# The sample tile's expert rows: eight single-row transfers on each of the SP and ACT queues in place of two indirect transfers on GpSimd

## The chip, the cores and the metric

The kernel runs on one core of one Trainium2 chip. The metric is the device time of one execution in microseconds (us); lower is better.

## The reference, cut to what matters

One inference step of a decoder trunk with two layers, for 512 prompt tokens and 8 sample tokens that share every weight, all in float32, model width 1024. Each layer is a mixer (mLSTM in layer 0, differential attention over a paged cache in layer 1, memory attention beside both), an output projection, a layer norm, a hierarchical mixture of 16 experts and a second layer norm. The change touches only what lies around the experts:

```python
ffn = hier_moe(x, w_group, b_group, w_router, b_router, w_e1, w_e3, w_e2)
return layer_norm(ALPHA * x + ffn, ln_ffn_g, ln_ffn_b)

def hier_moe(...):
    lg = xt @ w_group + b_group                      # 4 groups
    g = argmax(lg); p_g = softmax(lg)[g]
    le_g = (xt @ w_router + b_router)[group g]       # 4 experts of the group
    vals, idx = top_k(le_g, 2)
    wk = softmax(vals) * p_g                         # two experts a token, with weights
    h = silu(xt @ w1[e]) * (xt @ w3[e])
    y = sum over the two chosen e of wk * (h @ w2[e])
```

## The kernel before, in words

The 520 tokens lie in SBUF in `X` as five tiles of the token rows: tiles 0 to 3 are the prompt's, 128 rows each, and tile 4 (`PT`) is the samples' with 8 rows. `ORDER` is `[4, 0, 1, 2, 3]`, so that the samples' tile comes first wherever tiles are walked. Five engines each run their own list of instructions in written order (PE, VectorE or DVE, ScalarE or ACT, GpSimd or POOL, and SyncE or SP, which only issues transfers), and semaphores tie them together. The program is cut into blocks, and all five engines meet between two blocks: nobody begins the next block before the last one has ended this one.

The stages of a layer that matter here:

- **Routing** (`route(l, R)`, a block of its own). DVE works out, for each token, the two rows (`SLU`, `q` = 0 and 1) of a DRAM buffer `XS` in which the token's vector is wanted, since `XS` is ordered by expert, and raises `slot_ready`. GpSimd then scatters the five tiles of `X` to `XS` with ten indirect transfers, two for each tile (L1209), each of which counts into `xs_out`. ACT and DVE meanwhile work out the weights `WT2` of the two experts: ACT takes two exponentials (L1193, L1195), and DVE ends with L1309 to L1315. In layer 0 the same block also holds the memory keys and values of layer 1: PE multiplies them, ACT copies four banks out (L1200) and a transposed one (L1202), and SP stores them to DRAM (L1157, L1158) once four copies are there (`mem1_out`), and waits for these two stores (`mem1_kept`) at the end of its block.
- **Experts** (`experts(l, R)`, in the next block). ACT waits for `xs_out` and then loads `XS` in groups of 128 rows (`rows_in`, L1398). PE transposes each group (L1348), multiplies it with the experts' weights (L1359, L1381), and the results go to a second DRAM buffer `YS`.
- **Combination** (`combination(l, R)`). When every row of `YS` is written, ACT raises `y_all` (L1530). SP then loads the norm's scale and shift (`GB`, L1566), GpSimd gathers the tokens' rows back from `YS` into `YG` with ten indirect transfers (L1572), two for each tile in the order of `ORDER`, each pair counting into `ys_in[t]`. For each tile ACT scales the first row by its weight (`weigh`, L1580), DVE adds both rows to the residual (`residual`, L1625 to L1628), ACT takes the deviation (`deviation`, L1587, L1588) and DVE applies the norm (`normed`, L1635 to L1637). DVE's order is residual(0), residual(1), normed(0), residual(2), normed(1), and so on; ACT's is weigh(0), weigh(1), deviation(0), weigh(2), deviation(1), and so on, and index 0 is the samples' tile.

After the combination of layer 0 the same block goes on with layer 1: PE first turns the samples' tile and projects it, then the prompt's tiles, and the SP queue loads weights and cache pages (L1922, L1940, L1947). After the combination of layer 1 only the stores of the output are left.

## Time and profile before

| | us |
|---|---|
| median of 3 runs | 1326.72 |
| the three runs | 1319.88, 1326.72, 1330.5 |
| the profiled execution, its own time | 1322.12 |
| its span in the trace | 1320.3 |
| PE busy | 1101.7 (83% of the span) |
| DVE busy | 395.9 (30%) |
| ACT busy | 259.8 (20%) |
| POOL busy | 57.7 (4%) |

PE is busy most of the time, and the moments in which it is not are the places where the change acts: around the two scatters and the two combinations. The busy share of an engine therefore says little here; what counts is the wait that ends last at each of these four places.

### The profile page before, as it was taken

To read this page: it belongs to the slowest core of one execution; us is meant where nothing else is said; L and a number is where in the kernel's file an instruction comes from. 1 tells how busy PE (TensorE), PEld (TensorE's weight loads), DVE (VectorE), ACT (ScalarE), POOL (GpSimd) and SP (SyncE) were. 2 spreads that over 40 slices of the span, in tenths; PEclk is the share of its full clock that TensorE was granted. 3 is DMA by queue.
4 is the path that set the end of the run, shared out by engine and by line. 5 is a ranking of instruction groups with operands and counts; after the bars stand their busy time and mean duration, and the time that the engine had idled before them with its cause. 6 is when DMAs were issued, how large, how long until landed. Compare 5 with 4: busy or idle time off the path is not lost. (4 is left out here: it accounts for less than half of the span.)

```text
span 1320.3 us, 22081 instructions
## 1 busy us (share of the span) xinstructions
PE 1101.7 (83%) x8836; PEld 689.5 (52%) x8836; DVE 395.9 (30%) x1034; ACT 259.8 (20%) x686; POOL 57.7 (4%) x75
## 2 busy tenths in 40 slices
PE   7899999968994999917999888998876993699860
PEld 5688888854454333306887755554543442233210
DVE  2132223333534111136010023344333336011118
ACT  2122222113011111133110022223342101111014
POOL 4000000000002000030000000000000002000012
PEclk9999999979998899968999889999877997799885
DMA  9944442155626999999999955999623704899934
GB/s 335 407 151 120 120 120 81 45 172 227 272 103 246 343 400 410 339 337 319 356 351 351 340 178 186 351 358 353 251 106 119 287 0 186 312 374 374 420 127 187
DMA packets 131414, 333.91 MB, mean 253 GB/s; under 512 B 9951, under 2 KB 67472, under 8 KB 121710
## 3 DMA queue, kind: packets, MB, share of 16 engines
q1 hardware_dynamic: 115630, 274.98, 57.8%
q0 software_dynamic: 9200, 34.39, 6.6%
q10 hardware_dynamic: 6480, 23.10, 4.5%
q8 instruction: 71, 1.16, 0.3%
q14 instruction: 33, 0.27, 0.1%
HBM read 288.25 MB, written 44.19 MB: 252 GB/s over the span
## 5 line engine op out<-in xcount | busy, mean ns | idle before, releaser
L1359 PE MATMUL bank<-W,XT 128*32 128x512 f32 x1408 | 160.9, 610 | 6.3 <-DMA W<-in_w13f 3.9
L2141 PE MATMUL bank<-XT,W 128*128 128x260 f32 x448 | 113.1, 409 | 4.7 <-DVE CAT L2399 3.2
L1071 PE MATMUL bank<-WOUT,CAT 128*128 128x512 f32 x256 | 111.6, 594 | 0.0
L2141 PEld LDWEIGHTS bank<-XT,W 128*128 128x128 f32 x448 | 88.5, 203 | 27.6 <-issue 8.2
L1359 PEld LDWEIGHTS bank<-W,XT 128*32 128x32 f32 x1408 | 44.9, 113 | 106.8 <-issue 103.2
L485 PE MATMUL bank<-XT,WH 128*128 128x260 f32 x448 | 100.0, 384 | 0.0
L485 PEld LDWEIGHTS bank<-XT,WH 128*128 128x128 f32 x448 | 84.5, 190 | 13.3
L485 PE MATMUL bank<-WH,XT 128*128 128x256 f32 x384 | 84.0, 379 | 0.0
L1381 PE MATMUL bank<-WD,GT 128*32 128x512 f32 x704 | 80.0, 595 | 1.6 <-DVE GT L1455 1.6
L1071 PEld LDWEIGHTS bank<-WOUT,CAT 128*128 128x128 f32 x256 | 48.0, 190 | 57.9 <-issue 57.8
L485 PEld LDWEIGHTS bank<-WH,XT 128*128 128x128 f32 x384 | 72.5, 190 | 10.0 <-issue 0.4
L1348 PE MATMUL bank<-C,CAT 128*128 128x128 f32 x176 | 25.8, 293 | 42.0 <-DMA CAT<-XS 42.0
L1447 DVE TENSOR_TENSOR XT<-bank,XT 128x256 f32<-128x256 f32 x22 | 9.3, 424 | 161.0 <-ACT XT L1422 161.0
L1992 PE MATMUL bank<-PGS,QD 128*32 128x128 f32 x1536 | 48.6, 279 | 6.1 <-DMA PGS<-in_KP 6.1
L1348 PEld LDWEIGHTS bank<-C,CAT 128*128 128x128 f32 x176 | 20.3, 148 | 59.2 <-DMA CAT<-XS 42.5
L2081 PE MATMUL bank<-PGS,CAT 128*32 128x384 f32 x512 | 47.3, 491 | 4.2 <-DMA PGS<-in_VP 4.2
L1992 PEld LDWEIGHTS bank<-PGS,QD 128*32 128x32 f32 x1536 | 41.5, 112 | 14.1 <-issue 12.6
L2141 PE MATMUL bank<-WV,XT 128*128 128x256 f32 x192 | 45.8, 394 | 1.7 <-ACT XT L987 1.7
L1381 PEld LDWEIGHTS bank<-WD,GT 128*32 128x32 f32 x704 | 20.8, 109 | 45.7 <-issue 43.7
L1209 POOL DMA_INDIRECT XS<-X,SLU x20 | 19.0, 949 | 524.8 <-DVE SLU L1292 519.3
L2141 PEld LDWEIGHTS bank<-WV,XT 128*128 128x128 f32 x192 | 36.8, 196 | 8.0 <-ACT XT L987 1.8
L1422 ACT ACTIVATE XT<-bank 128x256 f32<-128x256 f32 x22 | 8.5, 385 | 157.9 <-PE bank L1359 157.9
(401 smaller groups left out, 1275.5 us busy)
## 6 DMA issues: line engine op xcount, KB each, us to landing
W<-in_w13f SPq DMA_DIRECT2D x32, 2048.0 KB, 12.7
PGS<-in_KP SPq DMA_DIRECT2D x128, 384.0 KB, 5.2
PGS<-in_VP SPq DMA_DIRECT2D x128, 384.0 KB, 5.2
WD<-in_w2f SPq DMA_DIRECT2D x32, 1024.0 KB, 13.6
WH<-in_w_a SPq DMA_DIRECT2D x13, 1024.0 KB, 11.1
CAT<-XS ACTq DMA_DIRECT2D x22, 512.0 KB, 10.0
XS<-CAT POOLq DMA_DIRECT2D x19, 512.0 KB, 15.5
WOUT<-in_w_out SPq DMA_DIRECT2D x4, 2048.0 KB, 13.1
```

The lines of the kernel that those rows point to most:

```text
L485: last = nc.tensor.matmul(PB[u["bank"]][:, 0:u["w"]], u["lhsT"](w, k), u["rhs"](w, k), start=(k == 0), stop=(k == KC - 1))
L1071: last = nc.tensor.matmul(PB[2 * (i % 2) + c][:, :], CAT[:, k, t * P:(t + 1) * P], w_out(c)[:, k, :], start=(k == 0), stop=(k == KC - 1))
L1209: nc.gpsimd.indirect_dma_start(XS, bass.IndirectOffsetOnAxis(ap=SLU[0:rows(t), q, t:t + 1], axis=0), X[0:rows(t), t, :], None).then_inc(xs ...
L1348: last = nc.tensor.transpose(PB[k // 4][:, (k % 4) * P:(k % 4 + 1) * P], XG[:, g % 3, k * P:(k + 1) * P], ident)
L1359: last = nc.tensor.matmul(PB[2 + g % 2][32 * j:32 * j + 32, :], XGT[:, g % 2, k, 32 * j:32 * j + 32], W13[:, LANES[l][g][j] % WRING, k, :] ...
L1381: last = nc.tensor.matmul(PB[5 + c][32 * j:32 * j + 32, :], GT[:, g % 2, k, 32 * j:32 * j + 32], WD2[:, LANES[l][g][j] % WRING, k, c * 512 ...
L1422: nc.scalar.activation(SIL[:, g % 2, :], PB[2 + g % 2][:, 0:FE], ACT.Silu).then_inc(s_ready, 1)
L1447: nc.vector.tensor_tensor(GA[:, g % 2, :], PB[2 + g % 2][:, FE:2 * FE], SIL[:, g % 2, :], ALU.mult).then_inc(g_ready, 1)
L1992: last = nc.tensor.matmul(bank[32 * j:32 * j + 32, q * P:(q + 1) * P], QD[:, i, 4 * g + j, :], page[:, j, i, :], start=(i == 0), stop=(i = ...
L2081: last = nc.tensor.matmul(PB[6 + c][32 * j:32 * j + 32, 0:384], weight, v, start=(p == 0), stop=(p == PAGES))
L2141: last = nc.tensor.matmul(PB[u["bank"]][0:u["m"], 0:u["w"]], u["lhsT"](w, k), u["rhs"](w, k), start=(k == 0), stop=(k == KC - 1))
```

## The change

The samples' tile leaves GpSimd. Its 16 rows (8 tokens, two experts each) are moved by 16 plain transfers of one row of 4 KB, eight on SP (q = 0) and eight on ACT (q = 1), whose DRAM row is a number that the engine has read from `SLU` into a register. GpSimd keeps the eight indirect transfers of the four full tiles, at the scatter and at the gather. New semaphores `xs_rows` and `ys_rows` count the single rows; who waited for `xs_out` or `ys_in[4]` now waits for these. The wait for the norm's scale and shift (`ln_in`) moves from ahead of residual(0) to ahead of normed(0).

The first `sample_rows` stands in `route`, the second in `combination`:

```diff
+            def sample_rows(eng, q):
+                eng.wait_ge(slot_ready, l + 1)
+                for b in range(NB):
+                    slot = eng.value_load(SLU[b:b + 1, q, PT:PT + 1], min_val=0, max_val=ROWS - 1)
+                    eng.dma_start(XS[bass.ds(slot, 1), :], X[b:b + 1, PT, :]).then_inc(xs_rows[q], 16)
...
                 def _(sp):
+                    sample_rows(sp, 0)
                     if l == 0:
                         sp.wait_ge(mem1_out, 4)
...
                 def _(act):
+                    sample_rows(act, 1)
                     act.wait_ge(rt_exp, 2 * l + 1)
...
                     pool.wait_ge(slot_ready, l + 1)
-                    for t in ORDER:
+                    for t in range(PT):
...
-                act.wait_ge(xs_out, 160 * (l + 1))
+                act.wait_ge(xs_out, 32 * PT * (l + 1))
+                for q in range(2):
+                    act.wait_ge(xs_rows[q], 16 * NB * (l + 1))
...
+            def sample_rows(eng, q):
+                slots = [eng.value_load(SLU[b:b + 1, q, PT:PT + 1], min_val=0, max_val=ROWS - 1) for b in range(NB)]
+                eng.wait_ge(y_all, l + 1)
+                for b, slot in enumerate(slots):
+                    eng.dma_start(YG[b:b + 1, 0, q, :], YS[bass.ds(slot, 1), :]).then_inc(ys_rows[q], 16)
...
             def on_sp(sp):
-                sp.wait_ge(y_all, l + 1)
+                sample_rows(sp, 0)
                 for c, name in enumerate(("ln_ffn_g", "ln_ffn_b")):
...
                 for i, t in enumerate(ORDER):
-                    for q in range(2):
+                    for q in range(2 if t < PT else 0):
...
-                    act.wait_ge(ys_in[t], 32 * (l + 1))
+                    rows_in(act, t)
...
+                sample_rows(act, 1)
                 weigh(0)
...
-                dve.wait_ge(ln_in, 64 * (l + 1))
                 residual(0)
                 for i in range(NT):
                     if i + 1 < NT:
                         residual(i + 1)
+                    if i == 0:
+                        dve.wait_ge(ln_in, 64 * (l + 1))
                     normed(i)
```

The next four listings show the order of instructions. In them `SLU_2710` is layer 0's `SLU`, `T_0_2692` the input of the first exponential, `SW_0_2700` that of the second, and ISA stands for register operations.

ACT in layer 0's routing block, before; the two copies from `bank` to XT and the two to MEMV are the memory keys and values:

```order
L1190 UNCONDITIONAL_BRANCH [waits barrier_Pool_Activation_PE_DVE_SP_release]
L1193 ACT_TABLE_LOAD
L1193 ACTIVATE T_0_2692<-T_0_2692 128x20 [waits rt_exp]
L1195 ACTIVATE SW_0_2700<-SW_0_2700 128x5 [waits rt_done]
L1200 ACTIVATE XT<-bank 128x256 [waits mem1_ready] x2
L1200 ACTIVATE MEMV<-bank 128x256 [waits mem1_ready] x2
L1202 ACTIVATE MEMKT<-bank 128x512 [waits mem1_ready]
```

The same place after the change, with the pair of value_load and transfer shown once of the eight times that it stands there:

```order
L1201 UNCONDITIONAL_BRANCH [waits barrier_Pool_Activation_PE_DVE_SP_release]
L1159 TENSOR_LOAD SLU_2710 [waits slot_ready]
L1159 ISA x2
L1160 ISA
L1160 DMA XS<-X 1x1024
...
L1205 ACT_TABLE_LOAD
L1205 ACTIVATE T_0_2692<-T_0_2692 128x20 [waits rt_exp]
L1207 ACTIVATE SW_0_2700<-SW_0_2700 128x5 [waits rt_done]
```

All eight rows, and the load of the activation table too, now stand between `slot_ready` and ACT's first exponential; the four copies for which SP's stores wait come behind them.

ACT from the end of layer 0's experts into its combination, before; L1530 is the instruction that raises `y_all`, and the tile YG is named YG_2939:

```order
L1530 ACTIVATE SW_0_2700<-SW_0_2700 1x1
L1580 ACTIVATE YG_2939<-YG_2939,WT_0_2711 8x1024 [waits ys_in4]
L1580 ACTIVATE YG_2939<-YG_2939,WT_0_2711 128x1024 [waits ys_in0]
L1587 ACTIVATE YG_2939,LNSF_2941<-X,LNSF_2941 8x1024 [waits var_ready]
L1588 ACT_TABLE_LOAD
```

After, where the value_load stands eight times and then the transfer eight times:

```order
L1544 ACTIVATE SW_0_2700<-SW_0_2700 1x1
L1585 TENSOR_LOAD SLU_2710
L1585 ISA x2
...
L1588 ISA [waits y_all]
L1588 DMA YG_3163<-YS 1x1024
...
L1607 ACTIVATE YG_3163<-YG_3163,WT_0_2711 8x1024 [waits ys_rows1,ys_rows0]
L1607 ACTIVATE YG_3163<-YG_3163,WT_0_2711 128x1024 [waits ys_in0]
```

On ACT the eight value_loads stand behind the instruction that raises `y_all`. On SP, which doesn't raise it, they stand ahead of the wait for it.

## Rows read from the trace of the kernel before

**Rows 1.** The list of waits: engine, line, awaited work; total us, times, longest

```profile
PE bank L1348 <- DMA CAT<-XS: 42.0, 2, 25.9
```

**Rows 2.** Timeline, layer 1, scatter: start, length, engine, line, operation, idle before

```profile
1112.70 0.17 DVE L1292 CAST SLU<-SW 128x10 uint32<-128x10 f32 x1
...
1113.19 0.95 POOL L1209 DMA_INDIRECT XS<-X,SLU  x1 [143.99 <-DVE SLU L1292]
...
1115.87 0.17 DVE L1309 TENSOR_REDUCE SW<-T 128x5 f32<-128x20 f32 x1
...
1117.03 0.17 DVE L1315 TENSOR_TENSOR WT<-WT,SW 128x5 f32<-128x5 f32 x1
...
1124.48 0.96 POOL L1209 DMA_INDIRECT XS<-X,SLU  x1 [0.30 <-issue]
1129.96 1.32 ACTq L1398 DMA_DIRECT2D CAT<-XS  x3
```

**Rows 3.** The stretches by windows, busy time of each engine, clock, DMA share, GB/s

```profile
421.00:424.00 3.00, 0.00 (x0) 0.00 (x0) 0.00 (x0) 0.00 (x0) 0.30 (x1) 0.50 1.01 388
```

**Rows 4.** SP's L1932 in 582.3 to 586 us, by source line

```profile
L1932 SPq TENSOR_LOAD <-PG x4: 260/274/283, 582.4 to 584.1; - x4
```

**Rows 5.** Timeline of SP, 614 to 616 us

```profile
614.22 1.90 SPq L1940 DMA_DIRECT2D PGS<-in_KP  x4
```

**Rows 6.** L1940 over the span, by source line: issue ns, and issue to landing

```profile
L1940 SPq DMA_DIRECT2D PGS<-in_KP x128: 332/333/2817, 591.7 to 750.4; - x128
...
DMA to landing us min/median/max: 3.0/5.2/10.5
```

**Rows 7.** Timeline, layer 0, scatter, columns as in rows 2

```profile
396.76 1.28 ACT L1193 ACT_TABLE_LOAD   x1 [0.57 <-PEq L1042]
...
408.58 0.17 DVE L1292 CAST SLU<-SW 128x10 uint32<-128x10 f32 x1
...
409.64 0.64 ACT L1200 ACTIVATE XT<-bank 128x256 f32<-128x256 f32 x2
...
410.17 0.38 ACT L1200 ACTIVATE MEMV<-bank 128x256 f32<-128x256 f32 x1
...
414.38 0.69 SPq L1158 DMA_DIRECT2D out_mem_v<-MEMV  x1
...
420.35 0.95 POOL L1209 DMA_INDIRECT XS<-X,SLU  x1 [0.30 <-issue]
426.88 1.31 ACTq L1398 DMA_DIRECT2D CAT<-XS  x3
```

**Rows 8.** L1158, the store of the memory values, issue to landing

```profile
DMA to landing us min/median/max: 6.4/6.4/6.4
```

**Rows 9.** Timeline, layer 1, combination, columns as in rows 2

```profile
1281.61 0.20 ACT L1530 ACTIVATE SW<-SW 1x1 f32<-1x1 f32 x1 [4.90 <-DMA YS<-CAT]
...
1287.97 1.15 ACT L1580 ACTIVATE YG<-YG,WT 8x1024 f32<-8x1024 f32 x1 [6.17 <-DMA YG<-YS,SLU]
...
1291.82 0.14 DVE L1628 TENSOR_SCALAR LNSF<-LNSF 8x1 f32<-8x1 f32 x1
...
1292.34 1.23 DVE L1625 SCALAR_TENSOR_TENSOR X<-X,YG 128x1024 f32<-128x1024 f32 x1 [0.39 <-ACT YG L1580]
...
1294.68 0.29 ACT L1588 ACTIVATE LNSF<-LNSF 8x1 f32<-8x1 f32 x1
...
1295.01 0.15 DVE L1635 RECIPROCAL LNSF<-LNSF 8x1 f32<-8x1 f32 x1
```

**Rows 10.** Timeline, layer 0, combination, columns as in rows 2

```profile
572.48 0.20 ACT L1530 ACTIVATE SW<-SW 1x1 f32<-1x1 f32 x1 [5.71 <-DMA YS<-CAT]
...
581.55 1.15 ACT L1580 ACTIVATE YG<-YG,WT 8x1024 f32<-8x1024 f32 x1 [8.87 <-DMA YG<-YS,SLU]
...
589.05 0.15 DVE L1635 RECIPROCAL LNSF<-LNSF 8x1 f32<-8x1 f32 x1
...
591.87 1.01 PE L979 MATMUL bank<-C,X 8*128 8x8 f32 x8 [25.77 <-DVE X L1637]
```

More of the change, by code:

```diff
@@ L1138, in _ @@
                             norm_steps(nc, dve, t, n0 + i, LNS, GB)
+        xs_rows = [sem("xs_rows0"), sem("xs_rows1")]
+        ys_rows = [sem("ys_rows0"), sem("ys_rows1")]
         rt_exp, rt_done, rk_in, rk_ready, slot_ready, xs_out = (
@@ L1561, in combination, with rows_in @@
             SLU, WT2 = R["SLU"], R["WT2"]
+            def rows_in(eng, t):
+                if t < PT:
+                    eng.wait_ge(ys_in[t], 32 * (l + 1))
+                else:
+                    for q in range(2):
+                        eng.wait_ge(ys_rows[q], 16 * NB * (l + 1))
+            def sample_rows(eng, q):
[3 more added lines that the diff above has]
+                    eng.dma_start(YG[b:b + 1, 0, q, :], YS[bass.ds(slot, 1), :]).then_inc(ys_rows[q], 16)
             def on_sp(sp):
-                sp.wait_ge(y_all, l + 1)
+                sample_rows(sp, 0)
                 for c, name in enumerate(("ln_ffn_g", "ln_ffn_b")):
@@ L1619, in residual @@
                     st = LNS[0:r, n % 2, :]
-                    dve.wait_ge(ys_in[t], 32 * (l + 1))
+                    rows_in(dve, t)
                     dve.wait_ge(y_weighed, NT * l + i + 1)
```

## The prediction

> **What bounds the kernel now.** I read the list of waits first. PE is the engine that does most of the work, so a change in a side path counts only where PE, or at the very end DVE, stands still for it. Twice, for 42.0 us together, PE waits for the first group of rows to come from XS, which can only be read when the scatter has landed [rows 1]. The timelines of the two scatters and the two combinations then show what ends last there. The four places are independent, so the result is the sum of four shifts.
>
> In layer 1's scatter the slots are ready at 1112.87 (the cast of 1112.70 and its 0.17). GpSimd issues its first transfer at 1113.19 and its tenth at 1124.48, one each 1.25 us, and ACT may issue the first load of XS at 1129.96 [rows 2]: 5.5 us behind the start of the tenth. In layer 0 the tenth is at 420.35 and the load at 426.88 [rows 7]; the DMA engines carry 388 GB/s between them [rows 3]. In the combinations the first thing that waits is ACT's scaling of the samples' tile, at 1287.97 and at 581.55; both end an idle time of ACT that was spent on the gather [rows 9, 10].
>
> **What one row costs.** The trace has both halves of it on SP. Four value_loads begin between 582.4 and 584.1, so one takes 1.7/3 = 0.57 us, of which the TENSOR_LOAD itself is 0.27 [rows 4]. Four transfers with an address in a register take 1.90 us; less the last one's 0.33, a third of the rest is 0.52 us each [rows 5, 6]. A scattered row therefore costs 1.09 us of its queue, eight rows 8.7 us. In the gather the loads come first (8 x 0.57 = 4.6 us) and then the transfers (seven steps of 0.52 = 3.6 us up to the start of the last). I take ACT to be as fast as SP; no row shows it. Against this, GpSimd needs 2 x 1.25 = 2.5 us for both transfers of the same tile.
>
> How soon a row of 4 KB lands is not in the trace. The shortest landing of L1940, of 384 KB, is 3.0 us and the median 5.2, in which the DMA engines are loaded [rows 6]. I take 3.0 where the queues are quiet and 4.0 where they are full.
>
> The Trainium skill, page "DMA: Bandwidth & Descriptors", speaks against this change: its section "Rules for kernel authors" says to coalesce many small transfers into one, since under 64 KB most of the time is overhead, and its section "Latency and other measured facts" puts the floor of a register load from a tensor at about 600 ns. The trace agrees with the second figure (0.57 us a value_load); with 0.6 for 0.57 the sum below would rise by 0.2 us in each combination.
>
> **Scatter, layer 1: -2.5 us.** GpSimd begins with tile 0 at once, so all eight full transfers and their data move 2.5 us forward: the last is issued at 1122.0 and the load of XS at 1127.4 [rows 2]. What must be over by then: the rows on both queues end at 1112.87 + 8.7 = 1121.6 and land 3 to 4 us later, 1125.6. ACT loads its activation table behind its rows (it did so at 396.76 in layer 0, during its wait, 1.28 us [rows 7]), and has its first exponential at about 1123.1. DVE's part that needs it took from 1115.87 to 1117.20, so 1.3 us [rows 2]; it ends at 1124.5. All this is covered by the landing of the scatter, with 2.9 us to spare for the slowest queue. If the drain of the data and not the issue set the end, nothing would be won; the bounds are -2.5 and 0, and I take -2.5, because GpSimd's first full tile is what starts the data.
>
> **Scatter, layer 0: 0 us.** GpSimd's side again ends 2.5 us earlier, at 424.4. But here the stores of layer 1's memory keys and values stand behind the rows. Step by step: slots ready 408.75; ACT's rows to 417.5; the table 1.28, to 418.8. From slots ready to the first copy, two exponentials included, it took 409.64 - 408.75 = 0.9, so the copies begin at 419.7; four of them are 0.64 + 0.38 + 0.38 = 1.4, to 421.1 [rows 7]. SP can then issue its two stores, the second some 0.5 us later (an estimate: one issue of 0.33 and a gap), at 421.6; in the trace it was issued at 414.38 and landed 6.4 us later in the midst of the scatter [rows 7, 8]. SP waits for it before the block may end. With 6.4 us the block ends at 428.0, with L1940's 3.0 at 424.6; half of the scatter's tail still lies beside it, so I take the middle, 4.7: 426.3, and 0.4 for the change of block. That is 426.7 against 426.88, no gain. Bounds: -2.5 if the store is hidden, +1.5 with its old landing.
>
> **Combination, layer 0: +2.6 us.** `y_all` comes from ACT's instruction at 572.48. Only behind it ACT does its eight value_loads, to 577.0, and begins the last row at 580.7 [rows 10]; SP has its loads done before and is 4 us ahead, so ACT is late. The DMA engines are full here: landed at 584.7, against the start of the scaling at 581.55, +3.1 us. From there to the reciprocal of the samples' tile it took 589.05 - 581.55 = 7.5 us, in layer 1 only 1295.01 - 1287.97 = 7.0 [rows 9, 10]; the 0.5 was tile 0's late arrival, and that is gone, since tile 0 is gathered 2.5 us earlier. PE starts on the samples' tile directly behind this norm, at 591.87 [rows 10], and all that follows hangs on it. DVE's later tiles follow in the same order and shift as well.
>
> **Combination, layer 1: +4.8 us.** Here the end of the kernel hangs on it. ACT's instruction is at 1281.61; loads to 1286.2, the last row begun at 1289.8, landed at 1292.8, against 1287.97 [rows 9]. DVE's first residual ends 4.0 us behind the scaling's start (1291.96), and before the change DVE then stood 0.4 us for tile 0 (1292.34); the deviation ends at 1294.97 and releases the reciprocal at 1295.01 [rows 9]. Behind the samples' tile all later tiles of DVE stand in a dense row, so the whole end moves: +4.8. The upper bound is a landing of 5.2 (+7), the lower one a value_load that costs its TENSOR_LOAD alone and transfers at 0.33, 8 x 0.27 + 7 x 0.33 = 4.5 us in place of 8.2: +1.1.
>
> **Without cost.** The wait for the norm's scale and shift: SP issues these loads about 4.2 us later (8 x 0.52), behind its rows. They are needed only by the first norm, which begins some 7 us after the scaling, so the move of the wait hides them. SP's loads behind them in layer 0 (WV, the pages) also start 4 us later into DMA engines that are full anyway.
>
> **Sum.** 0 - 2.5 + 2.6 + 4.8 = +4.9 us. Against the profiled execution's own time, 1322.12, that is 1327.0. That execution lies 4.6 below the median of 1326.72, and the mean of all four is 1324.8; on that I forecast **1330 us**, 0.4% slower.
>
> **Rivals.**
>
> *The samples' tile doesn't pace the combination.* If rows on ACT are as cheap as the lower bound and land at once, tile 0, which comes 2.5 us earlier, helps instead: -0.5 in layer 0 and -0.4 in layer 1 from the gaps that it left, and -2.5 in each scatter. Sum -5.9: 1319. For it: the engines' idle time before the scaling (8.9 and 6.2 us) was all wait for a transfer [rows 9, 10]. Against it: the loads are serial and behind `y_all`.
>
> *The scatter is bound by its drain.* The DMA engines carry 388 GB/s in the tail [rows 3], and one full tile of 512 KB each 1.25 us is 419 GB/s: more than they take. If the data and not the issue sets the end, GpSimd's 2.5 us come out of a queue that is full anyway, layer 1 gives 0 and layer 0 +1.5: sum +8.9, 1334.
>
> *Issuing a row is dearer than 0.52 us.* One issue of L1940 took 2.8 us where 0.33 is usual [rows 6], so an issue can be held up, and the rows are issued by SP and ACT at once while GpSimd's tiles flow. If a row's transfer costs p, each combination grows by 7(p - 0.52) and layer 0's scatter by 8(p - 0.52); layer 1's has 2.9 us to spare. At p = 0.9 the sum passes +13 us, the bound below; at p = 1.0 it is 4.9 + 6.7 + 3.8 + 0.9 = +16: 1341. Against it: the median of 128 issues is the shortest, 0.33.
>
> The Trainium skill, page "Perfetto Trace Analysis", section "DMA Instruction — HWDGE (DVE, Sync)", says that one descriptor generator is locked by one sequencer at a time and that this lock's wait is inside the profiled length. If SP and ACT share it, two streams of 0.33 us every 1.09 us (the scatter) fit into each other, and the sum stays.
>
> *The change does nothing.* Not possible for GpSimd's share; the four shifts could cancel to 0: 1325, inside the forecast's own range.
>
> **Chances.** The forecast (with what cancels) 0.57, drain-bound 0.18, not pacing 0.13, dear issue 0.12. A measurement of this kernel can tell about 1% from no change (the runs shown spread by 0.8%). 1% is 13.2 us: faster by that needs more than every gain in this sum, 0.03; slower by it is most of the last rival, 0.10; the rest, 0.87, is within. The range takes in the first rival and the second and stops short of the last: 1317 to 1340; of this, some 4 us at either end are the spread of the runs.
>
> **What would show it.** In the profile after: GpSimd's eighth indirect transfer 8.8 us behind its first at all four places; the rows of ACT 1.1 us apart in the scatter; ACT's load of XS at slots ready + 14.5 in layer 1 (17.1 before), and in layer 0 SP's end of the block released by the store of the memory values. In the combinations ACT's scaling of the samples' tile 11.2 us behind the start of ACT's L1530 in layer 1 (6.4 before) and 12.2 in layer 0 (9.1 before), released by a row, with tile 0 already there. I am wrong if ACT's value_loads cost clearly less than 0.57, if a row lands in under 2 us, or if the load of XS doesn't move in layer 1.

## The result, and the profile after

| | before | after |
|---|---|---|
| median of the runs, us | 1325.91 (4 runs, 1319.88 to 1330.5) | 1343.47 (4 runs, 1339.0 to 1347.73) |
| ratio after/before | | 1.0126, 95% interval 1.008 to 1.0171 |
| profiled execution, its own time | 1322.12 | 1347.73 |
| its span | 1320.3 | 1345.9 |
| PE busy / POOL busy | 1101.7 / 57.7 | 1109.8 / 48.4 |

The change makes the kernel 1.3% slower, 17.6 us; the forecast was 1330 us, 0.4% slower. The profiled execution is the slowest of its four, so its span of +25.6 us has to be taken apart. Length of each stretch in the two profiles, in us:

| stretch | before | after | difference | forecast |
|---|---|---|---|---|
| to layer 0's slots | 408.75 | 408.72 | 0.0 | 0 |
| layer 0, slots ready to PE's first group | 21.34 | 23.39 | +2.1 | 0 |
| layer 0, experts | 142.39 | 142.86 | +0.5 | 0 |
| layer 0, ACT's instruction behind the last store to PE on the samples' tile | 19.39 | 24.27 | +4.9 | +2.6 |
| from there to layer 1's slots | 521.00 | 530.39 | +9.4 | 0 |
| layer 1, slots ready to PE's first group | 20.54 | 20.24 | -0.3 | -2.5 |
| layer 1, experts | 148.20 | 149.88 | +1.7 | 0 |
| layer 1, ACT's instruction to the end of DVE's last norm | 35.66 | 43.12 | +7.5 | +4.8 |

The four places of the change give +14.1 us, each of them above its term. The 9.4 us between the layers can't be put down to the change: a second run of the same kernel had 513.96 there (E4 below).

The list of waits of the kernel after; columns as in [rows 1].

```profile
PE bank L1360 <- DMA CAT<-XS: 31.8, 2, 25.6
...
PE bank L979 <- DVE X L1665: 30.4, 1, 30.4
```

PE's wait for the rows of XS fell from 42.0 us [rows 1] to 31.8, and yet neither scatter won anything to speak of. In layer 0 the idle time is only split in another way: PE now stands 11.4 us for ACT's copy of the memory keys, which comes behind ACT's rows (row 424.81 of layer 0's scatter, below), does 1.1 us of transposes, and then stands 6.2 for XS. A group of waits that shrinks is no gain until the end of its stretch has moved. The second row grew by 4.6 us, and that is real [rows 10].

The timeline of layer 1's combination after, against [rows 9]:

```profile
1299.75 0.20 ACT L1544 ACTIVATE SW<-SW 1x1 f32<-1x1 f32 x1 [5.16 <-DMA YS<-CAT]
1300.13 3.21 SPq L1588 DMA_DIRECT2D YG<-YS  x8
1300.22 0.98 POOL L1599 DMA_INDIRECT YG<-YS,SLU  x1 [160.24 <-ACT SW L1544]
...
1304.16 3.28 ACTq L1588 DMA_DIRECT2D YG<-YS  x8
...
1308.98 0.94 POOL L1599 DMA_INDIRECT YG<-YS,SLU  x1 [0.30 <-issue]
1313.65 2.19 ACT L1607 ACTIVATE YG<-YG,WT 8x1024 f32<-8x1024 f32 x2 [13.70 <-DMA YG<-YS]
...
1320.61 0.15 DVE L1663 RECIPROCAL LNSF<-LNSF 8x1 f32<-8x1 f32 x1 [0.30 <-ACT LNSF L1615]
```

ACT's loads take 4.41 us (1299.75 to 1304.16), its rows 3.05 to the start of the last (1307.21), and then 6.44 us pass until the scaling. "x2" says that ACT scales the samples' tile and tile 0 without a gap: GpSimd's first full tile was there by the time ACT was free for it. The chain of waits has the same as "1307.21 6.36 DMA YG<-YS". From the scaling to the reciprocal it is 6.96 us, as before (7.04), and all later tiles follow. SP's loads of the norm's scale and shift are issued just ahead of ACT's rows and among them:

```profile
1303.38 0.37 SPq L1593 DMA_DIRECT2D GBF<-in_ln_ffn_g  x1
1304.10 0.36 SPq L1593 DMA_DIRECT2D GBF<-in_ln_ffn_b  x1
```

Layer 0's combination, the same view, against [rows 10]:

```profile
574.97 0.20 ACT L1544 ACTIVATE SW<-SW 1x1 f32<-1x1 f32 x1 [5.42 <-DMA YS<-CAT]
...
579.39 3.82 ACTq L1588 DMA_DIRECT2D YG<-YS  x8
...
589.46 2.19 ACT L1607 ACTIVATE YG<-YG,WT 8x1024 f32<-8x1024 f32 x2 [14.29 <-DMA YG<-YS]
...
599.24 1.02 PE L979 MATMUL bank<-C,X 8*128 8x8 f32 x8 [30.36 <-DVE X L1665]
```

The loads and the transfers of ACT's rows by source line (ns: shortest, median, longest):

```profile
L1585 ACTq TENSOR_LOAD <-SLU x16: 275/277/292, 575.0 to 1303.5; - x16
...
L1588 ACTq DMA_DIRECT2D YG<-YS x16: 226/235/510, 579.4 to 1307.2; - x16
```

In the gather the price of a row is as forecast or under it: a load each 0.55 us, a transfer each 0.41 in layer 1 and 0.48 in layer 0. In the scatter it is not. Layer 1's timeline after, against [rows 2]:

```profile
1129.46 0.17 DVE L1304 CAST SLU<-SW 128x10 uint32<-128x10 f32 x1
...
1130.52 12.52 ACTq L1160 DMA_DIRECT2D XS<-X  x8
...
1139.04 0.95 POOL L1221 DMA_INDIRECT XS<-X,SLU  x1 [0.30 <-issue]
1143.07 1.28 ACT L1205 ACT_TABLE_LOAD   x1 [26.08 <-issue]
1144.37 0.22 ACT L1205 ACTIVATE T<-T 128x20 f32<-128x20 f32 x1
...
1144.69 0.17 DVE L1321 TENSOR_REDUCE SW<-T 128x5 f32<-128x20 f32 x1 [12.05 <-ACT T L1205]
...
1145.75 0.17 DVE L1327 TENSOR_TENSOR WT<-WT,SW 128x5 f32<-128x5 f32 x1
1146.51 1.34 ACTq L1410 DMA_DIRECT2D CAT<-XS  x3
```

GpSimd's last transfer is issued 9.4 us behind the slots, where it was 11.6: of its forecast 2.5 us, 2.2 are there. But ACT's eight rows end 13.4 us behind the slots instead of 8.7; table, exponential and DVE's six steps on the weights stand behind them; and the block can't end until DVE is through. ACT's load of XS comes 16.9 us behind the slots (17.1 before). Layer 0 the same way, against [rows 7]:

```profile
409.64 12.93 ACTq L1160 DMA_DIRECT2D XS<-X  x8
...
422.60 1.28 ACT L1205 ACT_TABLE_LOAD   x1 [26.47 <-issue]
...
424.81 1.12 PE L1198 MATMUL bank<-C,XT 128*128 128x128 f32 x4 [11.36 <-ACT XT L1212]
...
425.79 0.48 SPq L1169 DMA_DIRECT2D out_mem_v<-MEMV  x1
...
428.80 1.35 ACTq L1410 DMA_DIRECT2D CAT<-XS  x3
```

The store of the memory values is issued at 425.79, 4.2 us later than I had it, lands 2.5 us later, and the block ends on it: the load is at 428.80, against 426.88.

### The profile page after: what moved, and what is told of

It is laid out like the page before. It is cut to its first block and busy times, and to the rows that moved or that the text cites. A ratio compares the mean times of both kernels' runs of the same rounds, so it can differ in the third digit from the quotient of the medians.

```text
span 1345.9 us, 22467 instructions
## 1 busy us (share of the span) xinstructions
PE 1109.8 (82%) x8836; PEld 692.9 (51%) x8836; DVE 396.2 (29%) x1034; ACT 259.0 (19%) x686; POOL 48.4 (4%) x67
## 3 DMA queue, kind: packets, MB, share of 16 engines
q10 hardware_dynamic: 6544, 23.24, 4.4%
q8 instruction: 71, 1.16, 0.3%
## 5 line engine op out<-in xcount | busy, mean ns | idle before, releaser
L2170 PE MATMUL bank<-XT,W 128*128 128x260 f32 x448 | 116.1, 417 | 4.7 <-DVE CAT L2428 3.2
L1360 PE MATMUL bank<-C,CAT 128*128 128x128 f32 x176 | 25.8, 293 | 31.8 <-DMA CAT<-XS 31.8
L2021 PEld LDWEIGHTS bank<-PGS,QD 128*32 128x32 f32 x1536 | 41.4, 112 | 16.8 <-issue 13.5
L979 PE MATMUL bank<-C,X 128*128 128x128 f32 (+1 forms) x120 | 16.0, 275 | 30.4 <-DVE X L1665 30.4
## 6 DMA issues: line engine op xcount, KB each, us to landing
W<-in_w13f SPq DMA_DIRECT2D x32, 2048.0 KB, 13.4
XS<-CAT POOLq DMA_DIRECT2D x19, 512.0 KB, 15.4
```

What stands on the lines that cost most here:

```text
L979: last = nc.tensor.transpose(PB[4 + 2 * (n % turns) + k // 4][:, (k % 4) * P:(k % 4) * P + r], X[0:r, t, k * P:(k + 1) * P], const("ident" ...
L1360: last = nc.tensor.transpose(PB[k // 4][:, (k % 4) * P:(k % 4 + 1) * P], XG[:, g % 3, k * P:(k + 1) * P], ident)
L2021: last = nc.tensor.matmul(bank[32 * j:32 * j + 32, q * P:(q + 1) * P], QD[:, i, 4 * g + j, :], page[:, j, i, :], start=(i == 0), stop=(i = ...
L2170: last = nc.tensor.matmul(PB[u["bank"]][0:u["m"], 0:u["w"]], u["lhsT"](w, k), u["rhs"](w, k), start=(k == 0), stop=(k == KC - 1))
```

## The experiments

Medians and ratios of all of them first; a ratio is given where there were several rounds, the rest are single runs.

| run | this, us | before in the same job, us | ratio, 95% interval |
|---|---|---|---|
| E1 scatter only | 1323.74 | 1323.4 | 0.9995, 0.9965 to 1.0025 |
| E2 gather only | 1336.81 | 1323.4 | 1.009, 1.0059 to 1.0121 |
| E3 before again | 1325.77 | 1323.4 | 0.9995, 0.9957 to 1.0033 |
| E4 after again | 1338.55 | 1323.4 | 1.012, 1.0049 to 1.0191 |
| E5 GpSimd's gather behind the rows | 1347.13 | 1326.21 | |
| E6 ACT's loads before the last stores | 1334.46 | 1326.21 | |
| E7 scatter only, exponentials first | 1327.09 | 1326.21 | |
| E8 scatter only, loads first | 1321.5 | 1326.21 | |
| E9 change with E6 and E7 | 1331.69 | 1322.43 | 1.0061, 1.0031 to 1.0091 |
| E10 scatter only, tiles held | 1334.53 | 1322.43 | |
| E11 scatter only, one queue | 1343.27 | 1322.43 | |
| E12 layer 1's scatter only | 1321.11 | 1322.43 | 0.9995, 0.9966 to 1.0023 |
| E13 as E9, loads inside the experts | 1327.5 | 1324.58 | 1.0022, 0.9999 to 1.0045 |
| E14 scatter only, tiles held, loads first | 1335.69 | 1324.58 | |
| E15 scatter only, tiles held, one queue | 1358.05 | 1324.58 | |

Single times of one kernel spread by 8 to 23 us, so the length of a stretch in each profile is the finer measure: scatter (slots to PE's first group) and combination (ACT's instruction to PE, or to DVE's last norm), in us.

| run | scatter 0 | combination 0 | between | scatter 1 | combination 1 |
|---|---|---|---|---|---|
| before | 21.34 | 19.39 | 521.00 | 20.54 | 35.66 |
| E3 | 21.43 | 19.59 | 521.09 | 20.33 | 35.80 |
| after | 23.39 | 24.27 | 530.39 | 20.24 | 43.12 |
| E4 | 23.48 | 24.28 | 513.96 | 20.24 | 43.65 |
| E1 | 23.24 | 19.34 | 518.95 | 19.44 | 35.75 |
| E2 | 21.29 | 24.16 | 525.32 | 20.31 | 43.10 |
| E5 | 23.57 | 29.66 | 524.77 | 20.26 | 44.27 |
| E6 | 23.14 | 19.14 | 524.26 | 20.05 | 37.53 |
| E7 | 22.06 | 19.48 | 524.16 | 19.05 | 35.76 |
| E8 | 22.22 | 19.40 | 519.22 | 20.47 | 35.69 |
| E9 | 22.21 | 19.36 | 524.17 | 19.05 | 38.39 |
| E12 | 21.36 | 19.61 | 520.81 | 19.12 | 36.04 |
| E13 | 22.13 | 19.02 | 528.50 | 19.16 | 37.76 |

### E1 to E4: the halves apart, and both kernels again

E1 takes the gather back (and the place of the wait for the norm's scale and shift with it), E2 the scatter; E3 and E4 are the kernels before and after, unchanged.

```diff
 E1
-                sample_rows(act, 1)        # in the combination, and on SP
-                    for q in range(2 if t < PT else 0):
+                    for q in range(2):
 E2
-                    sample_rows(act, 1)    # in the router, and on SP
-                    for t in range(PT):
+                    for t in ORDER:
```

> Only the two scatters are changed; the two combinations are as before. In the profiles, from the slots to PE's first group the changed kernel took 23.4 and 20.2 us, before 21.3 and 20.5. Theory A (the loss is the sum of the four places): the same two lengths again, +2 us in all, ratio 1.001 to 1.002, and PE's stretch from layer 0's combination to layer 1's slots 521 us as before. Rival B (the scatter change costs something elsewhere, since the stretch between the combination of layer 0 and the slots of layer 1 was 9 us longer in the profile after): +8 us or more, ratio 1.006 or more.

> Only the two gathers and the place of the wait for the norm's parameters are changed; the scatters are as before. Theory A: the combinations take 4.9 and 7.5 us longer than before, as in the profile after, so +12 us, ratio 1.009. Rival B: the gather change also lengthens the stretch after it, +17 us or more, ratio 1.013.

> The kernel before, profiled a second time, to see how much the lengths of stages vary from run to run. Theory A: the four changed places within 0.5 us of the first profile, while the stretch from layer 0's combination to layer 1's slots, where PE's granted clock fell to 0.73 and 0.83 in two windows, may vary by some 5 us on its own. Rival B: this stretch is 521 us again within 1 us, so that the 9 us in it belong to the change. Ratio 1.000.

> The changed kernel, profiled a second time. Theory A: 23.4, 24.3, 20.2 and 43.1 us at the four places again (within 0.5), and the stretch from layer 0's combination to layer 1's slots anywhere from 521 to 530. Rival B: that stretch is 530 us again. Ratio 1.010 to 1.014 in either case.

The whole measurable loss is the gather's: E2 costs 0.9%, some 12 us, and its two combinations are longer by 4.8 and 7.4, 12.2 together. E1 costs nothing that can be measured; its stretches give +1.9 and -1.1. The combinations repeat within 0.6 us from run to run. The stretch between the layers doesn't: E3 had the 521 us again that I had named as the sign of the rival, but E4, the changed kernel, had 514.0 where it first had 530.4, below all that I had expected. Over all 17 profiles it is 514.0 to 530.4.

A good part of the difference between the two profiles of the changed kernel is TensorE's clock. For the same 4151 matmuls of the stretch PE is busy for 456.6 us at a mean granted clock of 0.91 in the first and for 447.0 at 0.93 in E4, 9.6 of the 16.4 us. In the first, 40 us of it (999 to 1039) stand at 0.59, so mostly at the lower of the two levels, 1.2 and not 2.4 GHz; at the same place E4 has 0.87. Why the clock fell there in one run and not in the other stays open. Nor is it shown that the change has no part in this stretch: the seven profiles with the changed gather have 524.5 us on average, the ten others 520.7, a difference well inside their spread. E2's time, 12 us longer where its two combinations account for 12.2, speaks against a large one.

### E5 and E6: why a row lands so late

Theory: ACT's rows wait in the DMA engines behind the full tiles that GpSimd issues at the same time. Rivals: a row is slow by itself, or takes a constant 6.4 us. E5 lets GpSimd begin only when the rows have landed. E6 moves ACT's eight value_loads ahead of its wait for the last stores, so that the rows go out with fewer tiles ahead of them.

```diff
 E5
                 pool.wait_ge(y_all, l + 1)
+                for q in range(2):
+                    pool.wait_ge(ys_rows[q], 16 * NB * (l + 1))
 E6
                 count, done = number(act)
+                R["slots"] = [act.value_load(R["SLU"][b:b + 1, 1, PT:PT + 1], ...) for b in range(NB)]
                 for u in range(2):
                     act.wait_ge(y_stored[u], stored[u])
```

> The changed kernel, with GpSimd's gather of the four full tiles held back until the sixteen rows have landed. In both profiles after, ACT began the samples' tile 14.5 and 13.9 to 14.4 us behind L1544, of which the last row was issued at 7.5. Theory A (a row lands late because it is queued behind the full tiles that GpSimd issues at the same time): without them the last row lands 2 to 3 us behind its issue, so ACT begins at 9.5 to 10.5 us. Rival B (single rows are slow by themselves: 16 of them in 13.4 us, one after the other, 0.84 us each): ACT begins at 13.9 us again. In both the full tiles come later, so the combinations as a whole get longer; their length tells nothing.

> The changed kernel, with ACT's eight value_loads of the gather ahead of its wait for the last stores of YS, so that its rows are issued from L1544 on, 4.3 us earlier. Theory A (rows queue behind GpSimd's tiles): the last row is issued at about 3.9 us with three tiles' transfers ahead of it in place of six, and lands some 3 to 5 us later, so ACT begins at 7 to 9 us in place of 14, and the combinations are 5 us shorter. Rival B (rows are slow by themselves): the sixteen rows still take 13 us from the first issue, ACT begins at 13 to 14 us. Rival C (only ACT's lateness counts and the delay in the queue is constant, 6.4 us): ACT begins at 9.7 us, 4.3 earlier.

The timeline of E5, layer 1. GpSimd's first transfer now comes behind the scaling:

```profile
1298.00 0.20 ACT L1544 ACTIVATE SW<-SW 1x1 f32<-1x1 f32 x1 [4.91 <-DMA YS<-CAT]
...
1302.41 3.28 ACTq L1588 DMA_DIRECT2D YG<-YS  x8
1308.08 1.15 ACT L1609 ACTIVATE YG<-YG,WT 8x1024 f32<-8x1024 f32 x1 [9.88 <-DMA YG<-YS]
1308.83 0.98 POOL L1601 DMA_INDIRECT YG<-YS,SLU  x1 [169.77 <-DMA YG<-YS]
```

E6, layer 1:

```profile
1291.98 0.20 ACT L1545 ACTIVATE SW<-SW 1x1 f32<-1x1 f32 x1 [7.11 <-issue]
1292.36 3.28 ACTq L1589 DMA_DIRECT2D YG<-YS  x8
...
1300.28 2.19 ACT L1608 ACTIVATE YG<-YG,WT 8x1024 f32<-8x1024 f32 x2 [8.10 <-DMA YG<-YS]
```

The eighth row is issued 3.05 us behind the first. From there to the scaling it is 1308.08 - 1305.46 = 2.6 us without GpSimd's tiles, 1300.28 - 1295.41 = 4.9 with three of them issued before it, and 6.4 in the kernel after with six. So in layer 1 a row is not slow by itself, and it has no constant price. The rival of a constant 6.4 us would have put E6's scaling at 1301.8. E6 alone wouldn't show that it is the tiles, though: its rows are also issued ahead of SP's loads of the norm's scale and shift (1295.62, behind ACT's last row of 1295.41). E5 does, since it leaves these loads where they were, 0.78 us ahead of ACT's first row, and takes only the tiles away.

Layer 0 is another matter. There E5 gives

```profile
578.72 3.80 ACTq L1588 DMA_DIRECT2D YG<-YS  x8
...
580.18 5.53 SPq L1953 DMA_DIRECT2D WV<-in_w_kv  x3
587.21 1.15 ACT L1609 ACTIVATE YG<-YG,WT 8x1024 f32<-8x1024 f32 x1 [12.72 <-DMA YG<-YS]
```

The last row is issued at 581.88, so it takes 5.3 us to the scaling with none of GpSimd's tiles in flight, against 6.5 in the kernel after; ACT begins 12.9 us behind its instruction, where I had expected 9.5 to 10.5. E6 has 5.9 there, E13 (below) 5.8, little less than a constant delay would give. What stands beside the rows in layer 0 are SP's own transfers: between ACT's first and last packet the queue of SP moves 1.65 MB in E5: the norm's scale and shift and the weights that layer 1 needs first (WV). So GpSimd's tiles explain what is above 2.6 us in layer 1, and the smaller part of it in layer 0. No run takes SP's loads away; that they are the rest is argued from the packets, not shown.

The trace's records of single packets show how a row is held up. Start of ACT's packets, their length in us and their bytes, in layer 1's combination; the eight rows are issued at 1304.16 to 1307.21 in the kernel after and at 1302.41 to 1305.46 in E5:

```
kernel after               E5
1307.69 0.159 4096         1304.29 0.159 4096
1308.17 0.009    4         1304.69 0.009    4
1308.49 0.159 4096         1305.95 0.159 4096
1308.95 0.009    4         1306.11 0.009    4
1309.12 0.159 4096         1306.12 0.159 4096
...                        ...
1312.24 0.159 4096         1306.76 0.159 4096
1312.56 0.009    4         1306.91 0.009    4
1312.72 0.159 4096         1307.22 0.156 4096
1313.03 0.009    4         1307.38 0.009    4
```

A row is one packet of 4096 bytes with one of 4 bytes behind it, and the eight of a queue go one behind the other. In E5 six of them follow each other at 0.16 us, once the second has started, 1.7 us behind the first. In the kernel after it is 0.72 us a row (1307.69 to 1312.72 in seven steps): 0.15 to 0.3 us lie between a row's data and its 4 bytes, and 0.15 to 0.45 up to the next row, room for one to three packets of such a length from elsewhere each time. In these 5.3 us the core's 16 engines carry 320 packets (1.16 MB) of GpSimd's tiles and 211 (0.73 MB) of SP's queue, by their size the loads of the norm's scale and shift: six in ten of the neighbours are GpSimd's, four in ten SP's. ACT issues a row each 0.41 us, so they queue up: the first waits 3.5 us for its start, the last 5.5 (1.8 in E5); 0.3 to its 4 bytes and 0.6 to ACT's start make up the 6.4. So it is not one wait behind a mass of data but sixteen turns, each with others in between. The Trainium skill, page "DMA: Bandwidth & Descriptors", section "Queues, rings and completion order", says that each DMA engine takes the queues that have work in turn, packet by packet; the spacing of 0.72 against 0.16 us agrees. Which of the 16 engines a packet ran on is not in the records.

E5 as a kernel is worse than the change, since the full tiles now start late (combination 0: 29.66). In E6 the loss is gone in layer 0 (19.14, before 19.39) and down to +1.9 in layer 1. But ACT's instruction behind the last store is now held by the loads themselves ("<-issue"): 7.0 us behind that store (1285.00), 4.8 before the change. The experts' stretches carry this, 144.9 and 151.0 us where they were 142.4 and 148.2.

### E7 and E8: the scatter's order on ACT

Both start from E1. E7 puts ACT's rows behind the router's two exponentials, E8 does all eight loads first and then the eight transfers, as the gather has them.

```diff
 E7
-                    sample_rows(act, 1)
                     act.wait_ge(rt_exp, 2 * l + 1)
 ...
                     nc.scalar.activation(SW2[:, 0, :], SW2[:, 0, :], ACT.Exp).then_inc(rt_done, 1)
+                    sample_rows(act, 1)
 E8
-                for b in range(NB):
-                    slot = eng.value_load(SLU[b:b + 1, q, PT:PT + 1], min_val=0, max_val=ROWS - 1)
+                slots = [eng.value_load(...) for b in range(NB)]
+                for b, slot in enumerate(slots):
```

> Scatter changed alone (the gathers as before), with ACT's two exponentials ahead of its eight rows. Theory A (in layer 1 the block ended late because DVE's weights waited for the exponential behind the rows, DVE ending at slots + 16.3): the weights are done 12 us earlier, the block ends with the rows or with GpSimd's last, and PE's first group comes at slots + 17.5 to 19 in layer 1 in place of 19.4 and 20.2; in layer 0 the copies still stand behind the rows, 1.7 us earlier than with the change alone, so 21.5 to 22 in place of 23.3. Rival B (the landing of the scatter set the end anyway): layer 1 stays at 19.4 or above.

> Scatter changed alone (the gathers as before), with the eight value_loads ahead of the eight transfers, as in the gather. In the profile after one row took 1.6 us on ACT and 1.4 on SP, and its TENSOR_LOAD 0.77 and 0.56 us where it is 0.27 in the gather. Theory A (a TENSOR_LOAD behind a transfer of its own queue waits for it): loads first take 8 x 0.57 and the rows 8 x 0.5, together 8.6 us on ACT in place of 12.9. Rival B (the TENSOR_LOAD is slow because of what runs beside it, GpSimd's scatter and the other queue): they stay at 0.5 to 0.8 us, together 11 to 13 us.

The timeline of E7, layer 1; the slots are ready at 1117.99:

```profile
1119.45 12.82 ACTq L1160 DMA_DIRECT2D XS<-X  x8
...
1122.08 0.17 DVE L1327 TENSOR_TENSOR WT<-WT,SW 128x5 f32<-128x5 f32 x1
...
1133.77 1.34 ACTq L1410 DMA_DIRECT2D CAT<-XS  x3
```

DVE's weights are done 4.3 us behind the slots and hold nothing up; the load of XS comes 15.8 us behind them, 1.3 before its old place. PE's first group comes at 19.05, a hair above the 17.5 to 19 that I had expected. So half of the forecast 2.5 us is there once DVE's dependence is taken off. Not all of it is E7's: E1, whose scatter is the change's, had 19.44 in its own profile. What ends the block in E7 is GpSimd, whose last instruction there (DRAIN, L1162) ends 0.7 to 0.9 us behind the last packet of its tiles in every profile. This wait ends 15.4 us behind the slots, ACT's queue is through at 14.5 and DVE at 4.5. GpSimd's last tile is issued 2.2 us earlier than in the kernel before (9.4 and 11.6), but takes 6.1 us from there to the end of this wait instead of 5.2; with the rows out of the way (E10, E14, E15 below) it takes 5.1. So the rows beside the tiles cost the tiles 0.9 us.

In E8 the rival was right: the loads stay slow, and ACT's rows end only a little sooner (11.6 to 12.7 us behind the slots, E1 12.8 to 13.7). Layer 1 wins nothing, 20.47: GpSimd's wait for its tiles ends 16.8 us behind the slots. All the rows are issued late there, from 5.8 us on, and beside the last tiles; that this is what holds the tiles up is not shown. Its time of 1321.5 is one run and says nothing.

### E9 and E13: the change mended

E9 is the change with both mends, E6's and E7's. E13 moves ACT's loads further forward, into the experts' loop, three groups of tokens before its end.

```diff
 E13
                 for g in range(NG):
+                    if g == NG - 3:
+                        R["slots"] = [act.value_load(R["SLU"][b:b + 1, 1, PT:PT + 1], ...) for b in range(NB)]
```

> The changed kernel with both mends: ACT's value_loads of the gather ahead of its wait for the last stores (e6), and its exponentials ahead of its rows in the scatter (e7). If the loss lies where the theory puts it, lengths of the four places: layer 0 scatter 22.1 (before 21.3), layer 0 combination 19.1 (19.4), layer 1 scatter 19.1 (20.5), layer 1 combination 37.5 (35.7): +1.0 us in sum, so ratio 1.000 to 1.002, against 1.012 of the change. Rival (something of the gather change costs outside its place, for instance SP's loads of the next stage that are issued later): 12 us of loss shrink by the 10 that the places give back only in part, ratio 1.005 or more.

> As e9, but ACT's eight value_loads of the gather stand three groups before the end of the experts, where ACT waits some 7 us for PE in each group, in place of behind its last store of YS. In e6 and e9 ACT raised y_all 7.0 us behind that store (before 4.8 to 5.6), released by nothing but its own instructions. Theory: 5 to 5.6 us again, so the two stretches of the experts are 1.5 to 2 us shorter each than in e9 (145.2 and 152.6), the combinations at 19.2 and 37.5, and the ratio falls from 1.006 to 1.001 to 1.003. Rival (the rest of e9's loss has another cause): ratio 1.005 or more with y_all at 5 to 5.6 us.

E9 missed what I expected: 1.0061. Its loads came where ACT has no spare time: ACT's instruction is at 1290.41, 7.0 us behind the last store (1283.43), and the experts' stretches are 145.2 and 152.6 us (142.4 and 148.2 before). In E13 it waits for the store's landing again:

```profile
1288.99 0.20 ACT L1546 ACTIVATE SW<-SW 1x1 f32<-1x1 f32 x1 [4.88 <-DMA YS<-CAT]
1289.37 3.28 ACTq L1590 DMA_DIRECT2D YG<-YS  x8
...
1297.52 2.19 ACT L1609 ACTIVATE YG<-YG,WT 8x1024 f32<-8x1024 f32 x2 [8.33 <-DMA YG<-YS]
```

The experts take 142.2 and 147.5 us, and the ratio is 1.0022, as expected, with an interval that just reaches no change. What is left is layer 1's combination, +2.1: even with no load in front, the scaling comes 8.5 us behind ACT's instruction, 6.4 in the kernel before. Of these 2.2 us, 1.7 are issue, since the last of the eight rows goes out 3.4 us behind the instruction and GpSimd's second transfer of the samples' tile went out at 1.7 (1283.34); the landing from there takes 5.1 us instead of 4.6.

### E12: only where the profile shows a gain

E7 in layer 1 alone, everything else as before.

> What the places point to as the best version: of the whole change only the scatter of layer 1 is kept, with ACT's exponentials ahead of its rows; layer 0 and both gathers are as before. Theory: layer 1's scatter 19.05 us in place of 20.5 as in e7, all else as before, so 1.3 us or 0.1% faster, which the timed rounds can't tell from nothing: ratio 0.997 to 1.001 with an interval that holds 1. Rival: the interval excludes 1 on either side, and the places don't explain the time.

Layer 1's scatter is 19.12 us against 20.54, so 1.4 us are won in the profile. In the time they can't be seen: 0.9995, 0.9966 to 1.0023. No version beat the kernel before by more than the noise.

### E10, E11, E14, E15: why a scattered row costs 1.5 to 1.7 us

All start from E1. E10 holds GpSimd's tiles until the rows have landed, E11 puts all 16 rows on SP's queue and none on ACT's, E14 is E10 with all loads first, E15 is E10 with one queue. The data moved are the same; only order and queue change.

```diff
 E10
                     pool.wait_ge(slot_ready, l + 1)
+                    for q in range(2):
+                        pool.wait_ge(xs_rows[q], 16 * NB * (l + 1))
 E11
                     sample_rows(sp, 0)
+                    sample_rows(sp, 1)
 ...
-                    sample_rows(act, 1)
```

> Scatter changed alone, with GpSimd's eight full tiles held back until all rows have landed, so that the value_loads and row transfers run with nothing of GpSimd's beside them, both queues at once as in the change. In the scatter a TENSOR_LOAD took 0.72 us and a row 1.5 us, in the gather 0.27. Theory A (GpSimd's scatter beside them slows them): TENSOR_LOAD at 0.27 to 0.3, a row at 1.1 us or less, the eight in 8 to 9 us. Rival B (the two queues slow each other): 0.6 to 0.8 us, and 12 us for the eight, as in the change. The scatter as a whole gets longer by some 10 us; that tells nothing.

> Scatter changed alone, with all sixteen rows on SP and none on ACT; GpSimd's full tiles run beside them as in the change. Theory A (GpSimd's scatter slows the loads): a TENSOR_LOAD 0.6 to 0.8 us and a row 1.4 us again while GpSimd works, nearer to 1.1 once its data are through. Rival B (the queues slow each other): TENSOR_LOAD at 0.27, a row at 1.1 us from the first on. The scatter gets longer in both, 16 rows being 17 to 22 us.

> Scatter changed alone, GpSimd's tiles held back as in e10 and the value_loads ahead of the transfers as in e8, both queues at once. Theory A (two causes add up: what runs beside the loads, and a transfer just ahead of a load on the same queue): TENSOR_LOAD at 0.27 as in the gather, eight rows in 8 to 9 us. Rival B (the two queues slow each other whatever else runs): 0.4 us or more.

> Scatter changed alone, GpSimd's tiles held back and all sixteen rows on SP, each load ahead of its transfer. In e10 (two queues, tiles held) a TENSOR_LOAD took 0.54 to 0.60 us, in e11 (one queue, tiles beside it) 0.58. Theory A (a load behind a row transfer of its own queue is slow by itself): 0.4 us or more here too. Rival B (only the other queue or GpSimd's tiles slow it): 0.27 us and a row at 1.0 to 1.1 us.

The loads by source line (ns: shortest, median, longest), the kernel after:

```profile
L1159 ACTq TENSOR_LOAD <-SLU x16: 462/768/1131, 408.7 to 1141.1; - x16
```

E10, tiles held:

```profile
L1159 SPq TENSOR_LOAD <-SLU x16: 293/597/696, 403.7 to 1124.4; - x16
L1159 ACTq TENSOR_LOAD <-SLU x16: 291/544/647, 403.7 to 1124.5; - x16
```

E14, tiles held and loads first:

```profile
L1158 SPq TENSOR_LOAD <-SLU x16: 265/269/476, 410.5 to 1122.8; - x16
L1158 ACTq TENSOR_LOAD <-SLU x16: 273/276/477, 410.5 to 1122.6; - x16
```

E11, one queue with the tiles beside it, up to 1138 us and from 1140 on:

```profile
L1159 SPq TENSOR_LOAD <-SLU x8: 297/769/907, 1126.7 to 1136.8; - x8
L1159 SPq TENSOR_LOAD <-SLU x7: 495/572/593, 1140.2 to 1148.1; - x7
```

E15, tiles held, one queue:

```profile
L1159 SPq TENSOR_LOAD <-SLU x32: 297/570/579, 403.5 to 1147.3; - x32
```

E10's loads came out between its theory (0.27 to 0.3) and its rival (0.6 to 0.8), and the other three settle why. Two causes add up. A load that stands right behind a transfer of its own queue takes 0.54 to 0.60 us where one behind another load takes 0.27 (E10 and E15 against E14); the other queue has no part in it, since E15 has only one and pays the same. GpSimd's tiles beside it add some 0.15 to 0.2 more: 0.77 after and 0.72 in E1 on ACT's queue, and in E11 0.77 while the tiles run and 0.57 behind them. They slow loads-first rows as well (E8: medians 0.52 on SP, 0.40 on ACT, against 0.27 in E14). Eight transfers behind each other took 3.2 us in E14, as in the gather. What these kernels cost as a whole (scatters of 27 to 40 us) is the holding of the tiles or the doubled row of SP, and was known in advance.

## Why the prediction was wrong

Direction, places and path were right: four places, ACT as the late queue, the gather as the loss. Both terms of the combination were too small, the gain of layer 1's scatter was not there, and layer 0's scatter, put at nothing, was a loss; the range ended 3.5 us short of the median.

- **Combination, layer 1, +4.8: measured +7.5.** The step that failed is "I take 3.0 where the queues are quiet and 4.0 where they are full", for how soon a row lands. The loads took 4.4 us (forecast 4.6) and the transfers 3.05 (3.6), both a bit better. The landing was 6.4 us in place of 3.0. E5 shows the main reason: in this very place GpSimd has issued six tiles before the last row, and without them the landing is 2.6 us. The paragraph "Without cost" looks only at who waits for SP's loads of the norm's scale and shift; their data run beside ACT's rows (four in ten of the packets above), which may be a second reason and isn't shown, since no run takes them away. I called layer 1's queues quiet; the change itself fills them at that moment. The bound that I gave, 5.2, was read from landings without eight single rows in a queue, so it was no bound.
- **Combination, layer 0, +2.6: measured +4.9.** The same step: 6.5 us in place of 4.0 (the last row at 582.99, the scaling at 589.46). Here the tiles are the smaller part of it: 5.3 us remain without them (E5), and how much of that is SP's loads stays open. The 0.5 us from tile 0's gap came back as I had it.
- **"They are needed only by the first norm, ... so the move of the wait hides them."** Right: no wait for the norm's scale and shift shows in any of the profiles.
- **Scatter, layer 1, -2.5: measured -0.3.** GpSimd's share came nearly as forecast. The step that failed is "a scattered row therefore costs 1.09 us", put together from a load among loads and a transfer among transfers. Interleaved it is 1.5 on SP and 1.7 on ACT, so ACT's eight rows end 4.7 us later than I had them (13.4 behind the slots, not 8.7), past "2.9 us to spare". The end was set by DVE's weights behind ACT's exponential, on the path that I had described; E7 takes that off and wins 1.5 us of the 2.5. The rest goes into the landing of the tiles, 0.9 us longer beside the rows, which the forecast had unchanged. That the load of XS hardly moved (16.9 us behind the slots, 17.1 before) was one of the signs of being wrong that I had named.
- **Scatter, layer 0, 0: measured +2.1.** The chain rows, table, copies, stores, end of the block was right link by link; the rows' price moved its start, and the last store was issued 4.2 us later than forecast; it landed in 2.5 us and not 4.7, which gave half of that back.
- **The rivals.** "Issuing a row is dearer than 0.52 us" was right for the scatter and wrong for the gather, where it put its price: 0.41 us there. "Bound by its drain" put layer 1's gain at 0, which E7 and E12 refute with 1.5 and 1.4 us; but in both it is GpSimd's wait for its data that ends the block, so the rival is right on the path and wrong on the price. "The samples' tile doesn't pace the combination" is refuted by both timelines. None of the rivals had the landing as its mechanism, and the two landings lie 5.9 us above their terms, of the 9.2 us that the sum lacks.
- **The rules that spoke against the change.** The Trainium skill, page "DMA: Bandwidth & Descriptors", section "Rules for kernel authors", has small transfers coalesced, and E2's +0.9% agrees. Its floor of about 600 ns for a register load (section "Latency and other measured facts") is what a load behind a transfer took, 0.57 us; one among loads took 0.27, or 0.55 with its register operations.

The four places explain +14.1 us, and the ratio's interval is +10.6 to +22.7, so the difference of the medians, 17.6, needs no further cause, though it doesn't exclude one of a few us. E2's stretches and ratio (12.2 and 12 us) agree more closely.

## What to carry to other kernels

Before a bulk transfer is split into single rows on other queues, ask what will be in the DMA engines when the last small one is issued: its landing counts from there, and neighbours that the same event releases are ahead of it. Price an operation from rows in the same neighbourhood; a load between loads and a load behind a transfer differ by two. Whatever comes first in the queue of the bulk transfers, as the samples' pair did here, has a place that is lost when it moves to a queue of its own: in layer 1 the pair was there 4.6 us behind its last issue, the rows in 4.9 to 6.4. Look as well for transfers that hold nobody up themselves and run beside such a row; whether they cost it something was not tested here.

## What the runs showed of the hardware that I had not expected

- A 4 KB row with its address in a register is one packet of 4096 bytes and one of 4, 0.16 us a row in the quiet end of E5's layer 1, and 0.72 beside GpSimd's full tiles and SP's loads; issue to start of the packet is 0.9 to 1.1 us at the quietest (the first two rows of layer 0 in E5, E6 and E13).
- A TENSOR_LOAD takes 0.27 us behind another load and 0.57 behind a row's transfer of its own queue; GpSimd's indirect transfers at the same time add some 0.15 to 0.2.
- An indirect transfer of GpSimd takes 1.2 us of issue with 8 rows and 1.25 with 128, so leaving out two of ten brought the last issue forward by 2.2 us, but took off only 64 of 4160 KB.
- Rows beside GpSimd's full tiles delay these too: from the last tile's issue to the end of GpSimd's wait for its data it is 6.1 us in E7's layer 1, 5.2 in the kernel before, and 5.1 with the rows already landed (E10, E14).
- The same kernel had 514.0 and 530.4 us in the stretch between the layers in two of its runs, more than all four places of the change together; 9.6 us of it are the same matmuls at a mean granted clock of 0.91 in place of 0.93. Why the clock differed stays open.
